# Self-attention denominators halved between VectorE and quads, and the memory/gMLP stage laid out anew

## The reference

```python
def rms_norm(x, g):
    return x * rsqrt(mean(x * x, -1) + 1e-6) * g
h = rms_norm(x, norm_mix)
q, k, v, zg, qm, gate_logits = split(h @ w_in, [1024, 256, 256, 1024, 512, 6144])
# A: 8 query heads on 2 key/value heads of 128, all 8192 keys
y_attn = self_attention(rope(rms_norm(q)), rope(rms_norm(k)), v) @ w_attn_o
# B: zg = gelu(zg); u, v = split(zg); chunks of 128 tokens, 4 channel groups
mixed = einsum('gij,bcjgd->bcigd', w_s, rms_norm(v)) + b_s
y_gmlp = (u * mixed) @ w_gmlp_o
# C: 4 heads of 128 against 256 memory tokens
km, vm = split(rms_norm(mem) @ w_mem_kv)
y_mem = softmax(rms_norm(qm) @ rms_norm(km).T / sqrt(128)) @ vm @ w_mem_o
g_a, g_g, g_m = split(sigmoid(gate_logits), 3)
x = x + (g_a * y_attn + g_g * y_gmlp + g_m * y_mem) @ w_out
x = x + square(relu(rms_norm(x) @ w_ffn_up)) @ w_ffn_down
```

## Time and profile before

| | before |
|---|---|
| median of 3 runs | 2621.13 us (2618.53 to 2769.03) |
| profiled execution | 2621.09 us |
| span of the slowest core (4) in it | 2619.5 us |
| PE busy | 2446.6 us (93%) |
| PEld busy | 1057.0 us (40%) |
| DVE busy | 1204.4 us (46%) |
| ACT busy | 956.4 us (37%) |
| chain that ended last | PE 77%, DVE 11%, issue 5%, ACT 4%, DMA 2% |

### The profile page before, as it was taken

How to read it: one execution, slowest core, us unless ns; L and a number is a source line. 1 busy time by engine, 2 the same in 40 slices (tenths; PEclk the granted TensorE clock), 3 DMA queues, 4 the chain that set the end, 5 groups by cost and what they waited for, 6 DMA issues and landing times.

```text
span 2619.5 us, 33703 instructions; the slowest of 8 cores (2605.6 to 2619.5 us)
## 1 busy us (share of the span) xinstructions
PE 2446.6 (93%) x11621; PEld 1057.0 (40%) x11852; DVE 1204.4 (46%) x1756; ACT 956.4 (37%) x1243; POOL 51.0 (2%) x100
## 2 busy tenths in 40 slices
PE   5999989999999996679999998999999999999998
PEld 2444433333333332234444443444444444444443
DVE  2666688999898865742222221342112212211121
ACT  3666468988888854341111111211001001100100
POOL 1000000000000000000000000000000000000000
PEclk9999999999999998889999999999999999999999
DMA  9999240000000041314435348415343433433442
GB/s 185 187 183 184 57 91 9 25 20 22 25 17 1 1 97 33 65 33 82 79 65 93 69 73 178 100 37 97 77 85 65 88 73 66 95 65 74 88 97 97
DMA packets 27431, 201.40 MB, mean 77 GB/s; under 512 B 2944, under 2 KB 3200, under 8 KB 15104
## 3 DMA queue, kind: packets, MB, share of 16 engines
q0 software_dynamic: 13824, 153.26, 32.0%
q1 hardware_dynamic: 13440, 45.97, 5.3%
HBM read 344.09 MB, written 8.39 MB: 135 GB/s over the span
## 4 chain that ended last, share of the span: by engine, by line
PE 77%; DVE 11%; issue 5%; ACT 4%; DMA 2%; DVEq 0%; POOL 0%; ACTq 0%; SPq 0%; POOLq 0%
PE psum L288 75%; DVE arena L305 8%; ACT arena L302 3%; DVE arena L326 1%; DMA arena<-xT_own 1%; DMA arena<-xT_all 1%; ACT L302 1%; PE psum L439 1%; DVE arena L329 1%; PE psum L766 1%; PE psum L292 0%; DVE arena L322 0%; DVEq L156 0%; DVE arena L335 0%; POOL arena L285 0%
## 5 line engine op out<-in xcount | busy, mean ns | idle before, releaser
L288 PE MATMUL psum<-arena 128*128 128x512 bf16 (+2 forms) x10493 | 2386.3, 381 | 136.9 <-DVE arena L305 49.5
L288 PEld LDWEIGHTS psum<-arena 128*128 128x128 bf16 (+1 forms) x10724 | 1025.9, 100 | 1455.2 <-issue 347.1
L302 ACT ACTIVATE arena<-psum 128x1024 bf16<-128x1024 f32 (+2 forms) x806 | 673.2, 869 | 1246.4 <-PE psum L288 1189.7
L305 DVE TENSOR_TENSOR arena<-arena 128x1024 f32<-128x1024 f32 (+5 forms) x974 | 724.6, 744 | 451.0 <-ACT arena L302 354.6
L305 DVE TENSOR_TENSOR arena<-arena,psum 128x512 f32<-128x512 f32 x304 | 208.9, 688 | 794.4 <-PE psum L288 736.9
L302 ACT ACTIVATE arena<-arena 128x512 f32<-128x512 f32 (+7 forms) x186 | 162.3, 887 | 170.5 <-DVE arena L305 68.6
L302 ACT ACTIVATE arena<-psum,arena 128x256 f32<-128x256 f32 (+4 forms) x213 | 82.7, 433 | 52.9 <-PE psum L288 39.6
L326 DVE RECIPROCAL arena<-psum 128x128 f32<-128x128 f32 x96 | 87.6, 936 | 6.7 <-PE psum L288 5.6
L302 ACT ACT_TABLE_LOAD x38 | 48.8, 1283 | 75.5 <-DVE arena L305 27.7
L326 DVE RECIPROCAL arena<-arena 128x4 f32<-128x4 f32 (+4 forms) x63 | 26.0, 412 | 107.2 <-ACT arena L302 107.2
L322 DVE SCALAR_TENSOR_TENSOR arena<-arena 128x512 bf16<-128x512 f32 (+1 forms) x88 | 58.3, 697 | 1.0
(11 more groups left out here) (23 smaller groups left out, 52.0 us busy)
## 6 DMA issues: line engine op xcount, KB each, us to landing
arena<-wp POOLq DMA_DIRECT2D x16, 2048.0 KB, 14.8
arena<-wup POOLq DMA_DIRECT2D x16, 2048.0 KB, 13.3
arena<-wdn POOLq DMA_DIRECT2D x16, 2048.0 KB, 12.5
arena<-xT_all POOLq DMA_DIRECT2D x30, 1024.0 KB, 10.5
arena<-wq SPq DMA_DIRECT2D x16, 512.0 KB, 8.2
arena<-xT_own SPq DMA_DIRECT2D x16, 512.0 KB, 3.6
arena<-wout POOLq DMA_DIRECT2D x4, 2048.0 KB, 17.8
arena<-xT_own SPq DMA_DIRECT2D x8, 1024.0 KB, 34.8
```

The source lines that it names most:

```text
L288: P.add("pe", lambda e: e.matmul(out.ap, lhsT=lhsT.ap, rhs=rhs.ap, start=start, stop=stop), reads=[lhsT, rhs], writes=[out])
L302: P.add("act", lambda e: e.activation(out=out.ap, in_=in_.ap, func=func, **kw), reads=rds, writes=[out])
L305: P.add(eng, lambda e: e.tensor_tensor(out=out.ap, in0=in0.ap, in1=in1.ap, op=op), reads=[in0, in1], writes=[out])
```

## The change

In self-attention DVE adds the first tile of each pair, and every second tile goes to a quad: eight quads a unit instead of six. `acc` is one tile. The partition sum comes after pair 6 of the next unit, the reciprocals after 9, 11, 13 and 15, the product after 18; for the last unit they come after the first memory query projection.

In memory/gMLP the query and u projections go in passes of two query tiles and one u tile, with the memory tokens' squares in two of them; the other four u projections are put between the steps of the memory tokens. GELU is written with one STT in place of TS and TT. Memory attention is computed per token tile (`m_out`): tokens on the partitions, denominators by matmuls with a single column of ones, one RECIP of 128x4 and one TT, then a transpose (`m_tr`). Its steps are put between the v projections, and v's Sqrt is taken for four tiles at once. The second half of it (`hooks`) runs inside the first two iterations of the gate stage.

```diff
         acc = accw[ui % 2]
-        both = gp % 4 == 3
         if gp == 0:
-            COPY(acc[0], pb[0])
-        elif gp == 3:
-            TT(acc[0], acc[0], pb[0], ALU.add)
-            COPY(acc[1], pb[1])
-        elif both:
-            TT(acc.all(), acc.all(), pb.all(), ALU.add)
+            COPY(acc.all(), pb[0])
         else:
-            TT(acc[0], acc[0], pb[0], ALU.add)
-        if not both:
-            held.append(pb[1])
+            TT(acc.all(), acc.all(), pb[0], ALU.add)
+        held.append(pb[1])
...
         if len(held) == 4:
-            quad(lb, held, gp < 6, gp >= 28)
+            quad(lb, held, gp == 3, gp == NP - 1)
...
         if gp == NP - 1:
-            TT(lsum.all(), acc[0], acc[1], ALU.add)
-            TT(lsum.all(), lsum.all(), PS(lb), ALU.add)
+            TT(lsum.all(), acc.all(), PS(lb), ALU.add)
...
-            deferred = [(2 + 3 * i, f) for i, f in enumerate(mk())]
-    for _, f in deferred:
-        f()
+            deferred = list(zip((6, 9, 11, 13, 15, 18), mk()))
...
-        ACT(t1, src_ps, AF.Square)
-        TS(t1, t1, C1, ALU.mult, 1.0, ALU.add)
-        TT(t1, t1, src_ps, ALU.mult)
+        ACT(t1, src_ps, AF.Square, scale=math.sqrt(C1))
+        STT(t1, t1, 1.0, src_ps, ALU.add, ALU.mult)
...
+    def m_out(tt):
+        qt, o = tt // 4, (tt % 4) * 128
+        for h in range(4):
+            for mt in range(2):
+                p_ = pm_[qt * 4 + h][mt, o:o + 128]
+                MM(Ref(banks[4][:, h * 128:(h + 1) * 128], PS(4).gran), p_, vm[mt, h * 128:(h + 1) * 128], mt == 0, mt == 1)
+            for mt in range(2):
+                p_ = pm_[qt * 4 + h][mt, o:o + 128]
+                MM(Ref(banks[5][:, 256 + h:257 + h], PS(5).gran), p_, ones[0:1], mt == 0, mt == 1)
+        r = lr[tt % 2].all()
+        RECIP(r, Ref(banks[5][:, 256:260], PS(5).gran))
...
+    p3_mm(0)
+    for _, f in deferred:
+        f()
+    p3_post(0)
+    zu(0)
+    p3_mm(1)
+    p3_post(1)
+    for i in range(1, 4):
+        p3_mm(2 * i)
+        p3_tr(2 * i - 2)
+        p3_post(2 * i)
+        p3_mm(2 * i + 1)
+        p3_tr(2 * i - 1)
+        p3_post(2 * i + 1)
+        zu(i)
+        if i == 1:
+            mem_sq(0, 2)
+        elif i == 2:
+            mem_sq(2, 4)
     pool_dma(wzv.all(), wzv_d, "w_zv")
+    p3_tr(6)
+    mem_stat()
+    zu(4)
+    mem_norm(0, 8)
+    p3_tr(7)
+    zu(5)
+    mem_norm(8, 16)
+    mem_proj(0, 0)
+    zu(6)
+    mem_proj(1, 0)
+    zu(7)
+    mem_proj(0, 1)
+    mem_proj(1, 1)
+    k_mem_tr(0)
+    k_mem_tr(1)
+    w_first = ring_load(wp5_d[0])
+    for u in (0, 1):
+        m_scores(u)
+        m_exp(u)
+    zv_mm(0)
...
+    zv_mm(4)
+    m_tr(0)
+    m_out(1)
+    zv_post(4)
+    zv_ss(2)
...
+    hooks = {
+        (0, 0): [R(zv_ss, 5), R(zv_ss, 6), R(zv_ss, 7), R(zv_mix, 2), R(zv_mix, 3), R(m_out, 4), R(zv_root, 4, 8)],
+        (0, 1): [R(m_tr, 4), R(m_out, 5), R(zv_norm, 4), R(zv_norm, 5)],
+        (0, 2): [R(m_tr, 5), R(m_out, 6), R(zv_mix, 4), R(zv_mix, 5), R(zv_norm, 6), R(zv_norm, 7)],
+        (1, 0): [R(m_tr, 6), R(m_out, 7), R(zv_mix, 6), R(zv_mix, 7)],
+        (1, 1): [R(m_tr, 7)],
+    }
...
-        i = (2, 1, 0)[rslot[0] % 3]
+        i = (1, 0, 2)[rslot[0] % 3]
```

More of the change, by code:

```diff
@@ new lines, in mem_stat, with mem_norm, mem_proj @@
+    def mem_stat():
+        for c in range(16):
+            MM(PS(5, 256), ones.all(), msq[c], c == 0, c == 15)
+        ACT(mrs.all(), PS(5, 256), AF.Sqrt, scale=1.0 / D, bias=eps_col)
+        RECIP(mrs2.all(), mrs.all())
+    def mem_norm(lo, hi):
+        for c in range(lo, hi):
+            STT(memn[c], memT[c], g_mem(c), mrs2.all(), ALU.mult, ALU.mult)
+    KMB = [2, 5]
+    VMB = [6, 7]
+    def mem_proj(mt, half):
+        b = (KMB, VMB)[half][mt]
+        for c in range(16):
+            MM(PS(b), memn[c, mt * 128:(mt + 1) * 128], wmkv[c, half * 512:(half + 1) * 512], c == 0, c == 15)
+        if half == 0:
+            norm_heads(PS(b), g_mk, m3, qmn[mt].all())
+        else:
+            COPY(vm[mt], PS(b), eng="act")
@@ new lines, in zv_root, with zv_norm, zv_mix @@
+    def zv_root(lo, hi):
+        ACT(vsd[lo:hi], vss[lo:hi], AF.Sqrt, scale=1.0 / 512.0, bias=eps_col)
+        RECIP(vrs[lo:hi], vsd[lo:hi])
+    def zv_norm(tt):
+        STT(vn[tt % 2].all(), vg[tt].all(), vrs[tt:tt + 1], sgu.all(), ALU.mult, ALU.mult)
+    def zv_mix(tt):
+        n_ = vn[tt % 2]
+        pm = 6 + (tt % 2)
+        for g in range(4):
+            MM(Ref(banks[pm][:, g * 128:(g + 1) * 128], PS(pm).gran), n_[g * 128:(g + 1) * 128], wsT[g * 128:(g + 1) * 128], True, True)
+        TT(gtmp.all(), PS(pm), bsp.all(), ALU.add)
+        TT(gmT[:, tt * 128:(tt + 1) * 128], gtmp.all().v(lambda ap: ap.rearrange("p (g i) -> p g i", i=128)),
+           uT[:, tt * 128:(tt + 1) * 128], ALU.mult)
@@ L950, in interleave @@
-    def interleave(gens):
-        gens = [g for g in gens if g is not None]
-        while gens:
-            for g in list(gens):
-                try:
-                    next(g)
-                except StopIteration:
-                    gens.remove(g)
-    p4_mm(0)
-    for k in range(9):
-        if k + 1 < 8:
-            p4_mm(k + 1)
-        interleave([p4_h2(k - 1) if k >= 1 else None, p4_h1(k, gi + k) if k < 8 else None])
-    dump("gmT", gmT.all())
-    gs = [[B(44 + 6 * i + 2 * k, [512], F32) for k in range(3)] for i in range(2)]
@@ L967, in build @@
-    acc = [B(56 + 2 * i, [512], F32) for i in range(2)]
-    tmpm = [B(60 + 2 * i, [512], F32) for i in range(2)]
     rslot = [0]
     def ring_load(src_ap):
-        i = (2, 1, 0)[rslot[0] % 3]
+        i = (1, 0, 2)[rslot[0] % 3]
         rslot[0] += 1
@@ L985, in build, with gate @@
             i2 = it % 2
-            for br in range(3):
+            def gate(br):
                 gb = (it * 3 + br) % 2
@@ L1002, in build @@
                     TT(mergedT[c, tsl], acc[i2].all(), tmpm[i2].all(), ALU.add)
+            gate(0)
+            branch(0)
+            gate(1)
+            if it < 2:
+                gate(2)
+                branch(1)
+            else:
+                branch(1)
+                gate(2)
+            branch(2)
             it += 1
+    dump("memoT", memoT.all())
+    dump("gmT", gmT.all())
     dump("mergedT", mergedT.all())
```

193 lines of the change are left out of this document (91 added, 102 removed).

## The result

The changed kernel takes 2546.24 us, median of four runs beside runs of the kernel before at 2621.22: a ratio of 0.971, 95% interval 0.9683 to 0.9737, 75.0 us less. The prediction was 2556 (2533 to 2590), faster over 2% with a chance of 0.66. The sign and the stage's size were right; attention gave more than forecast and for another reason than the one I gave.

What follows compares the result with a forecast made beforehand. The prediction took the kernel as mostly PE-bound, so only stretches where PE waits could give time. Attention -14.9, tail -6.1, projections -19.5, memory keys and values +6.4, memory attention and gMLP v -31.4: -65.5 from 2621.1, 2556 us (2533 to 2590).

Steps and rivals of the forecast that it cites:

- Attention, the later sum: Self-attention: moving the partition sum from pair 2 to pair 6 removes PE's waits before it, -23.9 us.
- DVE just fits: Self-attention: DVE's work in a new unit, 33.8 us, fits within the unit's 34.4 us.
- Attention, quads: Self-attention: eight quads a unit for six, 32 more at 0.28 us each, cost +9.0 us.
- rival B: Whole kernel PE-bound: quads hidden and the memory/gMLP stage near its matmuls, 2537 us; chance 0.10.
- B's first half: Self-attention: the added quads cost nothing, all else as forecast, which alone gives 2547 us.
- Attention, size: Self-attention as a whole, added quads and removed waits together: -14.9 us.
- unexplained: Self-attention: about 0.3 us of the old unit without explanation, carried into the new unit's 34.4 us.
- Rival D: Self-attention: DVE takes over, units stay at 35.6 us and the 15 us are not gained, 2571 us; chance 0.09.
- Tail, projections, keys and values: Attention's end to memory keys and values: tail -6.1 us, projections -19.5 us, memory keys and values +6.4 us.
- Memory attention and gMLP v: Memory attention and gMLP v, with work moved into the gate stage: 60.2 us for 91.6, -31.4 us.
- Rival C: Memory/gMLP stage stays a chain of ACT and DVE, projections give half, 2578 us; chance 0.18.
- E: Memory/gMLP stage: small matmuls and waits hold TensorE at 1.2 GHz, slower, 2696 us if all at half clock; chance 0.03.

Runs made afterwards that it cites:

- j: The changed kernel with every key tile summed by TensorE, sixteen quads a unit and no adds of exp tiles on DVE: 2568.7 us (one run).
- f: The changed kernel with three PSUM banks in turn for the memory query projections instead of two: 2541.4 and 2544.8 us.
- l: The kernel before, with the reciprocals of memory attention's denominators replaced by copies: 2609.3 us (one run).
- e: The changed kernel with the steps woven into the first two gate iterations carried out before the first gate matmul instead: 2560.7 and 2560.5 us, ratio 0.9777.

## Why the prediction was right, and where it was not

**Attention, the later sum: wrong.** "The waits go: -23.9 us" is the step that failed. They went, but the later sum did not do it: by itself it gave 5.8 us with the old split, 4.3 of which were lost again behind the last quad, and none with the new. I read the row [28.5 <-DVE] of the earlier trace rows as a wait with a place, to be cured by moving the place. It was a load: DVE at 90% with self-waits between its adds. The relief, eight tiles a unit off DVE, stood in the sum at nothing ("DVE just fits"); it gave 18.8 to 24.7 up to the last quad, with the price of its own quads already off. That the number held all the same is luck: the change had both edits in it, and I priced the loss that went, not what made it go.

**Attention, quads: right in kind, too dear.** +9.0 us at 0.28. j prices one at 0.19 net, about 6 us for 32. That PE's pace in attention could be under 0.242 was rival B's ground, and the starts show it (0.216); but a quad costs 0.43 at that pace and was not free. B's 2537 did not come. That B's first half, 2547 with free quads and all else as forecast, is the measured time is a coincidence of a dearer quad and a larger relief of DVE. The Trainium skill's figure in "TensorE: Matmul & The Clock Gate" (Back-to-back issue gap), about 216 ns, is what the trace shows from start to start, in dense stretches (32 matmuls in 6.91 us, changed kernel, core 0, from 942.56) and within the pairs of attention. My 0.221 has the end of the last matmul in it, and my 0.242 the short waits between pairs, so I was wrong to say that the case does not agree in attention.

**Attention, size.** -14.9 forecast, about -25 measured, which is the whole of the miss (2556 against 2546.2). Units came out at 33.9 us (538.0 over 15.9 units) for my 34.4: four pairs and a quad at 4.07 to 4.18 for 4.15, and nothing left of the 0.3 "unexplained" (8 x 4.13 + 0.86 = 33.9). My own unit would have given -19.2 for 16 of them; I summed by single waits instead, and should have asked why the two differed.

**Rival D: wrong way round.** It feared that DVE would still hold the pace at 33.8 us a unit. DVE stands 55.7 us for ACT in the window, and its own need is 29.0 us a unit. The estimate took self-waits at their worst, 25 a unit; the changed kernel has 83 in 14 units, and 25.7 us of them in the window before became 14.3. It also added up mean records (29.3), which overlap: DVE is busy 385.2 / 14.19 = 27.1.

**Tail, projections, keys and values: right.** From attention's end to the first memory scores 113.5 us before, 94.3 forecast, 96.0 measured (916.7 to 1012.7). The wait for the reciprocals' bank is 0.19 us, the pass with squares 13.65 us from one Sqrt load to the next (14 forecast), and before the key projection PE stands twice, 3.20 and 2.01 us. I had not seen the 4.44 us for a bank of the query projections, but f shows that it is worth 1.0.

**Memory attention and gMLP v: right in sum, two errors inside.** From the scores to the first gate matmul 44.7 us (47.0 forecast), the two gate iterations 43.9 us for 29.5 before (+14.4, 13.2 forecast). The 16 small matmuls of `m_out` cost 0.63 us a tile, not 1.6: 3.98 us between 1044.26 and 1048.24 less 16 x 0.216 is 0.52 for 14 of them, and 0.11 for the two in front. The bank wait was 0.57 for 0.7. What this saved went into waits before the mixes (3.09, and 2.91 for a transpose's copy in the gate iterations) for which I had no term. Of the reciprocals, l shows 13.9 us, of the weave, e shows 14 to 17, and the GELU was up to twice my price. These overlap, so the sum of 50.0, for a forecast of 50.6, is better than its terms were.

**Rival C** (the stage stays a chain, 2578) did not come, **E** neither: the granted clock rose. e shows its mechanism in small, 30.7 us at 0.50. DMAs cost nothing, as said: no wait of PE for a weight block shows between 917 and 1101 us.

## What to carry to other kernels

An idle time with a releaser's name has a place and a cause, and they differ when the releaser is near 90% busy with waits on itself: look at whether *it* ever waits for its inputs. If not, its load is the bound, and moving the wait only changes who stands. Compare loads per unit of work, not shares of a window: a longer unit hides a heavier load. Price a dependent pair of instructions on a chain by the distance from first start to last end, not by the difference of records. Where PE stands for a short chain of small DVE and ACT work, put independent matmuls there: they hide it and keep the clock.
